# Presetting the merge-gate rows with their bias in HBM and adding the gate products to them by DMA

## The reference, cut to what matters

```python
h = layer_norm(x, ln_in_g, ln_in_b)
proj = h @ w_in[l]
(aq, ak, av, ag, bq, bk, bv, bf, bg, cq, cg, mg) = split_columns(proj)
...
branches = (oa * jax.nn.silu(ag), ob * jax.nn.silu(bg), oc * jax.nn.silu(cg))
merged = None
for n in range(N_BRANCH):
    gate = jax.nn.sigmoid(mg[..., n * D_MODEL:(n + 1) * D_MODEL] + b_gate[l, n])
    term = gate * (branches[n] @ w_branch[l, n])
    merged = term if merged is None else merged + term
y = merged @ w_out[l]
h = layer_norm(alpha * h + y, ln_g[l], ln_b[l])
```

## Time and profile before

| | us |
|---|---|
| median of 3 timed runs (1840.96 to 1842.37) | 1841.87 |
| the profiled execution, its own time | 1840.76 |
| its span | 1838.9 |
| PE busy in the span | 1822.7 (99%) |
| DVE busy | 1317.2 (72%) |
| ACT busy | 863.3 (47%) |
| POOL busy | 201.9 (11%) |
| TensorE's granted clock, mean | 0.997 |

### The profile page before, as it was taken

One profiled execution on the slowest core, in us unless ns is written; L12 is line 12 of the kernel. 1 busy time (PEld: TensorE's weight loads), 2 busy tenths in 40 slices (PEclk: granted clock), 3 DMA queues, 4 the chain that ended last, 5 costly groups with the idle time before them and its releaser, 6 DMA issues.

```text
span 1838.9 us, 24157 instructions
## 1 busy us (share of the span) xinstructions
PE 1822.7 (99%) x8577; PEld 1513.7 (82%) x8577; DVE 1317.2 (72%) x2086; ACT 863.3 (47%) x1458; POOL 201.9 (11%) x276
## 2 busy tenths in 40 slices
PE   9999999999999999999999999999999999999997
PEld 7888888888888888888888888888888888888885
DVE  5777764887777775566678878878788645566778
ACT  5653332545555554344445555555456333244643
POOL 1111110100212120000000000000001000002222
PEclk9999999999999999999999999999999999999998
DMA  9576676962643433444263451624527544439987
GB/s 330 182 206 177 186 198 214 237 218 66 178 122 94 117 101 110 118 116 140 69 193 106 170 189 53 217 69 161 201 75 285 184 149 149 149 115 238 245 211 176
DMA packets 226470, 299.38 MB, mean 163 GB/s; under 512 B 13585, under 2 KB 140625, under 8 KB 224337
## 3 DMA queue, kind: packets, MB, share of 16 engines
q1 hardware_dynamic: 171824, 188.24, 32.2%
q0 software_dynamic: 54416, 109.51, 22.2%
q10 hardware_dynamic: 144, 0.52, 0.1%
HBM read 247.73 MB, written 50.97 MB: 162 GB/s over the span
## 4 chain that ended last, share of the span: by engine, by line
PE 97%; DVE 1%; DMA 1%; ACT 0%; issue 0%; DVEq 0%; POOL 0%; POOLq 0%; SPq 0%; ACTq 0%
PE acc L668 10%; PE acc L670 10%; PE acc L669 10%; PE scores L863 6%; PE scores L861 6%; PE scores L859 6%; PE acc L863 3%; PE acc L861 3%; PE acc L859 3%; PE transposed L693 3%; PE scores L1104 2%; PE scores L1102 2%; PE scores L1103 2%; PE attended L863 2%; PE attended L861 2%; PE attended L859 2%
## 5 line engine op out<-in xcount | busy, mean ns | idle before, releaser
L1292 ACT ACTIVATE piece_split<-w 128x512 fp32r<-128x512 f32 x448 | 282.9, 633 | 288.4 <-PE scores L863 105.1
L1854 DVE TENSOR_TENSOR piece_split<-w,piece_split 128x512 fp32r<-128x512 f32 x448 | 309.1, 691 | 110.2 <-ACT piece_split L1292 98.5
L1708 DVE TENSOR_TENSOR w_lo<-raw_weights,w_hi 128x1024 fp32r<-128x1024 f32 x181 | 220.3, 1220 | 179.0 <-ACT w_hi L1187 177.7
L668 PE MATMUL acc<-h_hi,w_lo 128*128 128x512 f32 x800 | 319.3, 399 | 0.0
L670 PE MATMUL acc<-h_hi,w_hi 128*128 128x512 f32 x800 | 312.4, 391 | 0.0
L669 PE MATMUL acc<-h_lo,w_hi 128*128 128x512 f32 x800 | 311.7, 390 | 0.0
L1187 ACT ACTIVATE w_hi<-raw_weights 128x1024 fp32r<-128x1024 f32 x181 | 191.2, 1060 | 190.3 <-PE acc L1104 52.2
L670 PEld LDWEIGHTS acc<-h_hi,w_hi 128*128 128x128 f32 x800 | 150.2, 188 | 32.4
L668 PEld LDWEIGHTS acc<-h_hi,w_lo 128*128 128x128 f32 x800 | 150.4, 188 | 29.8 <-issue 1.8
L669 PEld LDWEIGHTS acc<-h_lo,w_hi 128*128 128x128 f32 x800 | 150.6, 188 | 28.5
L859 PE MATMUL scores<-piece_split,h_lo 128*128 128x512 f32 x384 | 149.6, 390 | 0.0
(11 more groups left out here) (447 smaller groups left out, 3675.3 us busy)
## 6 DMA issues: line engine op xcount, KB each, us to landing
w<-in_w_in SPq DMA_DIRECT2D x128, 512.0 KB, 7.4
raw_weights<-in_w_in SPq DMA_DIRECT2D x102, 512.0 KB, 3.9
raw_weights<-in_w_branch SPq DMA_DIRECT2D x48, 512.0 KB, 5.2
raw_weights<-in_w_mem_kv SPq DMA_DIRECT2D x32, 512.0 KB, 5.4
gate<-gate_scratch POOLq DMA_DIRECT2D x12, 1024.0 KB, 6.6
h_sums<-sums_scratch POOLq DMA_DIRECT2D x6, 1024.0 KB, 10.4
gate_scratch<-first_product POOLq DMA_DIRECT2D x12, 512.0 KB, 6.3
out_w_x<-in_w_out POOLq DMA_DIRECT2D x12, 512.0 KB, 8.4
```

What stands on the lines that cost most here:

```text
L668: pe.matmul(bank_out, wl, hi[:, k, :], start=first, stop=False)
L1292: act.activation(p_split[:, n % RING, 0, :], sources[p][:, k, :], ACT.Copy).then_inc(pc_hi, 1)
L1708: dve.tensor_tensor(w_lo[:, slot, :], raw[:, slot, :], w_hi[:, slot, :].bitcast(F32), ALU.subtract).then_inc(lo_ready, 1)
L1854: dve.tensor_tensor(p_split[:, n % RING, 1, :], sources[p][:, k, :], p_split[:, n % RING, 0, :].bitcast(F32), ALU.subtract).then_inc(pc_lo, 1)
```

## The change

Twelve new transfers (`preset_gates`) write the bias, each as 512 equal rows of 512 numbers, into the twelve parts of `gate_dram`: eight in the pairs of branch B, right behind `toep`, three in pairs 5 to 7 of branch A, and one behind that loop. `store_gate` of the gate groups adds its quarter to what stands in HBM instead of writing it. POOL waits, ahead of the first of these stores, until all presets have landed, and no longer ahead of the last layer norm. The twelve loads of the bias, the twelve additions on DVE with their semaphore and the two bias buffers go; ACT's tanh now waits for the gate load itself.

```diff
-    gate_bias = [at(R2 + 24576 + 2048 * b, f"gate_bias{b}", [P, 512], F32) for b in range(2)]
...
@@ act, step m, s == 2
-                        act.wait_ge(gate_biased, m + 1)
+                        act.wait_ge(gate_loaded[m % 2], 16 * (m // 2 + 1))
                         act.activation(gate[m % 2][:, :, :], gate[m % 2][:, :, :], ACT.Tanh, scale=0.5)\
                             .then_inc(gate_ready, 1)
...
@@ dve
-            def gate_rows(m):
-                dve.wait_ge(gate_loaded[m % 2], 32 * (m // 2 + 1))
-                dve.tensor_tensor(gate[m % 2][:, :, :], gate[m % 2][:, :, :],
-                                  gate_bias[m % 2][:, :].unsqueeze(1).broadcast_to((P, TT, 512)), ALU.add)\
-                    .then_inc(gate_biased, 1)
...
-                    if s == 1:
-                        gate_rows(m)
...
@@ pool, store_gate
                 if g < KV_GROUPS:
                     dst = kv_dram[g, 2 * half_t:2 * half_t + 2, :, half_n * 512:(half_n + 1) * 512]
+                    pool.dma_start(dst.rearrange("t p n -> p t n"), buf[:, :, :]).then_inc(done, 16)
                 else:
                     dst = gate_dram[n, nb, 2 * half_t:2 * half_t + 2]
-                pool.dma_start(dst.rearrange("t p n -> p t n"), buf[:, :, :]).then_inc(done, 16)
+                    pool.dma_start(dst.rearrange("t p n -> p t n"), buf[:, :, :], accum_op=ALU.add).then_inc(done, 16)
...
+            def preset_gates(k):
+                n, nb = k // 4, k % 4
+                rows = gate_dram[n, nb].rearrange("t p n -> (t p) n")
+                pool.dma_start(rows, b_gate[0][n, nb * 512:(nb + 1) * 512].partition_broadcast(SEQ))\
+                    .then_inc(preset, 16)
...
@@ pool, pair i of branch B, behind the toep transfer
+                preset_gates(i)
...
@@ pool, pair i of branch A
                 if i <= TT:
                     pool.dma_start(out_t[i - 1], ln_b[0].partition_broadcast(P)).then_inc(preset, 16)
+                else:
+                    preset_gates(PAIRS + i - TT - 1)
+            preset_gates(11)
             pool.wait_ge(multiplied, CH_M)
             load_s3()
...
+            pool.wait_ge(preset, 16 * (TT + 12))
             for g in range(KV_GROUPS, GROUPS):
                 store_group(g)
...
@@ pool, load_gate
-                    .then_inc(gate_loaded[m % 2], 16)
-                pool.dma_start(gate_bias[m % 2][:, :],
-                               b_gate[0][n, nb * 512:(nb + 1) * 512].partition_broadcast(P))\
                     .then_inc(gate_loaded[m % 2], 16)
...
-            pool.wait_ge(preset, 16 * TT)
             rstd(0)
```

More of the change, by code:

```diff
@@ L461, in program @@
         gate_loaded = [sem(f"gate_loaded{b}") for b in range(2)]
-        gate_biased = sem("gate_biased")
         gate_ready = sem("gate_tanh_ready")
@@ L653, in _ @@
             sp.dma_start(b2_row[:, :], ln_b[0].partition_broadcast(P)).then_inc(b2_loaded, 16)
-            sp.wait_ge(preset, 16 * TT)
+            sp.wait_ge(preset, 16 * (TT + 12))
             sp.wait_ge(last_half, 1)
```

## The result

The changed kernel takes 1845.68 us, the median of 12 runs (1844.02 to 1850.03); the kernel before 1840.90 us in the 12 runs beside them (1840.09 to 1842.37). The ratio is 1.0026, with a 95% interval of 1.0018 to 1.0033: 4.8 us slower. That is just past the 0.2% that the prediction called no change, and inside its range of 1838.5 to 1854. The profiled execution of the changed kernel is the slowest of its twelve, 1850.03 us, with a span of 1848.1 instead of 1838.9; its 9.2 us more are not the typical loss.

What follows compares the result with a forecast made beforehand. The prediction took PE, busy for the whole length of the three touched stages, as the bound. Its terms, 0 + 0 + 0 + 0 on 1841.87, gave 1841.9 us, no change (chance 0.73); the range was 1838.5 to 1854.

Steps and rivals of the forecast that it cites:

- rival 2: Gate groups 3 to 7: c21 adds land too late, PE waits for its fifth piece; 1846.7 to 1853.6 us, chance 0.11.
- What bounds the kernel: In branch B, gates and branch products PE is always busy; relieving DVE, ACT or POOL gains nothing unless PE waits.
- Bias additions and loads, price 0: Branch products: removing twelve DVE additions (27.4 us of DVE) and twelve 256 KB bias loads changes the time by 0.
- Rival 3: Branch products: less work on DVE shortens the stage after all, by up to 27.4 us, to 1814.5; chance 0.04.
- A preset costs 5.7 us: Each 1 MB preset, HBM to HBM, lands 5.7 us after issue, like the preset of `out` with `ln_b`.
- land 5 to 10 us after issue: Sign that the forecast is right: the presets land 5 to 10 us after they are issued.
- The presets of branch B, price 0: Eight presets behind `toep`: the values queued behind them still land in time for ACT's split, so 0 us.
- 522.80: Branch B, pair shown: latest time in us at which ACT's split of the values can begin without delaying anything.
- rival 1: Branch B: presets slow like `toep` make the values late, from 16 us a preset; 1866 or 1947 us, chance 0.09.
- The presets of branch A, price 0: Presets in branch A's loop, which already issued four transfers of the same size with `ln_b`, cost 0 us.
- The adds: Gate groups: 24 stores become adds, each landing 1.5 to 3.9 us later, 3.9 taken; PE not delayed, price 0.
- 11.85: Gate groups, c21 store: us after issue beyond which a later landing makes PE stand still; the add was put at 10.3.

Runs made afterwards that it cites:

- the wide rows: The changed kernel with each preset writing its 1 MB as 128 rows of 8 KB instead of 512 rows of 2 KB: 1841.79 us, ratio 1.0001.

## Why the prediction came out as it did

The forecast of no change was wrong by a little: the measured interval, 1.0018 to 1.0033, lies nearly all above its limit of 1.002. The range held the time, but by luck: it reaches above the forecast's own end, 1844, only for rival 2, which did not come and would have begun at 1846.7. Of the chance of slower, 0.23, no part was for late presets; nearest are the 0.03 for weight loads of SP held up, and there by the adds.

- **What bounds the kernel.** Right: PE is the bound, and nothing that the change takes from DVE or adds to POOL inside the stages is felt. The kernel with more work on DVE limits it: near the two ends of the branch products DVE has less than 4.6 us to spare in a step, and the 111 us of the stage don't show that.
- **Bias additions and loads, price 0.** Right. DVE is busy 131.97 us in the stage instead of 155.34, and the stage is as long. Rival 3 falls with it.
- **A preset costs 5.7 us.** Wrong, by a factor of about two: 10.4 to 10.9 in a quiet stretch, 13.7 by the median. I chose the row that had the same bytes and took the bytes for the price; that row is cut into 128 rows of 8 KB, and the wide rows show that the cut decides. The bound by `toep`'s rows, 19.4, was too high by nearly as much. So the sign "land 5 to 10 us after issue" failed for all twelve (10.4 to 19.3).
- **The presets of branch B, price 0.** Right, though they land 12.6 to 16.9 us after issue. They don't run behind `toep` but beside it (12.5 us for `toep` instead of 9.7), so the slowest, issued at 498.3, has landed by 515.2, ahead of the 522.80, though four of the eight take longer than the 16 us from which rival 1 was to decide. ACT and PE have no wait there that they didn't have before. Rival 1 stayed out.
- **The presets of branch A, price 0.** This is the step that failed. I argued that the same loop had carried transfers of that size, without looking at what else runs at the place of the last two. The four with `ln_b` lie in pairs 1 to 4; behind pair 7 SP loads weights of the first gate group, and one of those loads landed 2.0 us ahead of DVE's use and about 5 us ahead of the moment at which PE would feel it. It came 8.1 us later. The queue that I checked was POOL's; the one that was hit was SP's, on the same 16 engines. And two such presets decide it, not one. The price of the term is the wait of PE and the lower clock behind it, 3.1 + 2.9 us in the profiled execution, 2.6 + 1.7 in that with only the two late presets, where I had 0; the runs lose 4.8.
- **The adds.** The price was somewhat high for the store that matters: the adds of c21 land 9.1 to 9.5 us after issue in the five groups instead of 6.4 to 7.2, 2.1 to 2.7 more, where I took 3.9. (The medians, 9.1 and 6.3, mix c21 with c11.) That is short of 11.85, and in the kernel with the two presets moved PE has no wait in the gates. The Trainium skill, "Collectives: The Full Stack", section "The bandwidth ceiling: the fold count and why AG ≠ RS ≠ AR", has an adding transfer at about half the rate of a copy, for reductions between cores. Two stores come near that here. That of c22, the first of a group, takes 5.7 us now and

```profile
gate_scratch<-fifth_product POOLq DMA_DIRECT2D x6, 512.0 KB, 3.4
```

in the kernel before, 1.7 times; that of c11 3.7 to 4.1 us in the first five groups and 7.5 to 7.8 now, about twice, but it now begins while the add of c22 is still in flight. The later two rise less, c12 from 7.2 to 9.0 and c21 as above. So the store with the tight budget does not show a doubling of the landing time, which is what that rule of the Trainium skill would make of it, and rival 2 stayed out.

## What to carry to other kernels

A transfer that nobody waits for still has to be placed by what else is on the DMA engines, on every queue: find the loads with the least slack in the next twenty us, and put it where there are none. Count the slack up to PE: here 2.0 us to DVE's use and 3.0 more of split pieces. Where PE is the bound and never waits, the risk of a change lies not in the work it adds but in the one or two places with a few us of slack, and a wait there is paid beyond its length: the four of 2.5 to 9.9 us seen here cost another 1.7 to 2.9 us each by the clock. A large fill with a repeated row took half the time in long rows here.

## What the runs showed of the hardware

- 1 MB from HBM to HBM with a repeated row: 10.6 us as 512 rows of 2 KB, 5.5 us as 128 rows of 8 KB, in the same quiet stretch.
- A weight load of 512 KB, alone on SP's queue, lands in 3.5 us without the presets and took 13.4 with two of them in flight on POOL's queue; the load behind it took 11.9 instead of 3.8. From 939.0 to 944.4 SP's queue, with that load waiting on it, had 0.1% of the engines' time and POOL's 94.9%: in that stretch the two queues did not share the engines by halves.
- Waits of PE of 2.5, 2.6 and 9.9 us were followed by matmuls at the lower clock that cost 1.7 us each time, one of 3.1 us by 14 such matmuls, 2.9 us. Behind waits of 0.7, 0.8, 1.2 and 1.6 us the granted clock stayed at 1.00. Among these four waits the cost of the clock did not grow with the wait.
- An adding store of 512 KB from SBUF to HBM took 5.7 us instead of 3.4 as the first of its group, and 2.1 to 2.7 us more than a plain one for c21, beside weight loads.
